# A two-block network on one core: expert weights laid out in other runs, three result buffers, the router tile by tile, the first group by a product

## The chip, the cores and the metric

The program runs on one core of a Trainium2 chip. The metric is the device time in microseconds of one execution, median of three runs. TensorE (PE) multiplies matrices, its weight loads stand apart as PEld; VectorE (DVE), ScalarE (ACT) and GpSimd (POOL) compute; SyncE (SP) only issues transfers. GpSimd and ScalarE issue some too.

## The reference, cut to what matters

A first block of two layers (a mixer or attention and an MLP each, on 256 tokens and 256 context rows of width 1024) comes first and is not touched. The second block ends in the mixture of experts that the change is about. All is in float32.

```
h2 = _rms(x, norm2_g) * (1.0 + sc2) + sh2
g_logits = h2 @ w_rg + b_rg                       # 4 groups
g_top = argmax(g_logits); gate_g = softmax(g_logits)[g_top]
e_in = (h2 @ w_re + b_re).reshape(-1, 4, 4)[g_top]  # 4 experts of that group
top_v, top_j = top_k(e_in, 2)                     # 2 of them
w_sel = softmax(top_v) * gate_g
for e in range(16):
    he = silu(h2 @ w1[e]) * (h2 @ w3[e])          # w1, w3: 1024 x 512
    y += combine[:, e:e+1] * (he @ w2[e])         # w2: 512 x 1024
x = x + g2 * y
```

## The kernel before

Five instruction streams, one for each engine, are written out by hand and held together by semaphores. PSUM's eight banks go round in order of use up to the experts, and there have fixed roles. Weights come over SyncE's queue.

Behind the second block's output projection (`out_project(2, ...)`) VectorE adds the residual to each of two token tiles and norms it into `xn` (`rms_row`). TensorE transposes both tiles (`turn_x("moe")`), ScalarE and VectorE write the scaled and shifted columns to `hT` (`modulate`), with the scales and shifts in `modc`, one column for each block of 128 features. Then come the gates' broadcast (`gate_rows`) and the router's product. VectorE picks two experts for each token, TensorE counts how many tokens each expert has before each token ("pos"), and VectorE works out for each token and choice a slot, `slot_i`. An expert has a home of 64 slots; up to 7 spill units of 64 slots take what goes over, and `table_i` says for which expert each of them is.

GpSimd waits for `slot_i` and scatters the rows of `xn` into `x_slots` in DRAM with four indirect transfers (`x_spread`). Then it loads groups of 128 slots, two units, back into `xs`. `turn_group` transposes such a group, `modulate_group` scales it into `hs`. 23 units run in this order: expert 0, expert 1, spill 0, expert 2, expert 3, spill 1 and so on, and last 14 and 15. So a round is two experts and a spill unit. For each unit, `up` multiplies by w1 and w3 (32 passes of 128x512 on half the array), ScalarE and VectorE make silu and product, `turn_he` turns the result, `down` multiplies by w2 (16 passes) and `keep_y` scales it into one of two `ysb` buffers. GpSimd stores each in `y_slots`, and waits for two stores back guard the buffers. In the program every float32 product is two passes, two MATMULs in the profile.

SyncE loads w1 and w3 of an expert into two halves of `wring`, by the expert's parity, as soon as the `up` two experts back is done; w2 likewise into `w2_ring`. Spill units have buffers of their own, and their loads carry a condition, so one that isn't needed moves nothing. The first spill load waits for the table and for the scatters, since it writes over `xn`. It is SyncE's next one behind experts 0 and 1, so all weights behind it wait too. `inverse_roots` on GpSimd makes the inverse roots of all norms, in order with its transfers; two of them belong to the index keys at the start of the second block, which `rel_bias`, `w_rg` and other small loads precede.

The last two units' results are added by TensorE (`add_late`) with one-hot picks (`pick_late`, `turn_picks`); the others are gathered from `y_slots`.

## Time and profile before

| | us |
|---|---|
| median of 3 runs (1724.14 to 1730.26) | 1725.04 |
| profiled execution | 1726.32 |
| its span in the trace | 1724.5 |
| TensorE busy | 1626.6 |
| VectorE busy | 697.5 |
| ScalarE busy | 256.0 |
| GpSimd busy | 108.3 |

All times below are from the start of the span of the one profiled execution. The experts' part runs from about 1396 to the end. "busy" counts neither waits nor the issue of transfers. A row of the timeline gives start, length, engine, line and instruction, then in brackets the idle time ahead of it and what ended it; "issue" there is a wait that no semaphore event of an engine explains. SPq is SyncE's queue of transfers.

### The profile page before, as it was taken

What the parts mean: (1) busy time and instruction counts of PE and PEld (TensorE: products, weight loads), DVE (VectorE), ACT (ScalarE), POOL (GpSimd) and SP (SyncE); (2) the same over time, 40 slices, a digit from 0 to 9 for tenths busy, and PEclk for the clock granted to TensorE, in tenths of its full rate; (3) what the DMA queues carried; (4) which work ended last, traced back from release to release, by engine and by line L of the source; (5) the groups of instructions that cost most, each with busy time, mean ns of one, the idle gap of its engine ahead of it and who ended that gap; (6) DMA issues with size and microseconds to landing.
All of it is one profiled execution on the core that took longest, in us unless ns stands there. A gap on an engine that the chain in (4) does not pass through costs nothing.

```text
span 1724.5 us, 17356 instructions
## 1 busy us (share of the span) xinstructions
PE 1626.6 (94%) x6960; PEld 878.5 (51%) x6960; DVE 697.5 (40%) x1322; ACT 256.0 (15%) x576; POOL 108.3 (6%) x123
## 2 busy tenths in 40 slices
PE   4999999999999999999989999999989958998997
PEld 2445556474444444446756788448855633333332
DVE  1617853468886000112264765004484342111112
ACT  3121113010000000000154110000222311011110
POOL 1000001100000000001000100001131110110101
PEclk9999999999999999999989999999999978999999
DMA  9452441146665321107610699424623449999996
GB/s 340 169 195 99 146 165 56 49 147 219 214 225 207 135 98 49 49 1 257 225 50 1 229 333 363 175 98 154 197 98 122 147 178 354 390 392 391 391 387 254
DMA packets 160623, 333.94 MB, mean 194 GB/s; under 512 B 15288, under 2 KB 15568, under 8 KB 160544
## 3 DMA queue, kind: packets, MB, share of 16 engines
q1 hardware_dynamic: 141408, 298.90, 47.7%
q0 software_dynamic: 18224, 30.78, 5.5%
q10 hardware_dynamic: 912, 3.17, 0.5%
q8 instruction: 55, 0.90, 0.2%
q14 instruction: 24, 0.20, 0.0%
HBM read 355.02 MB, written 15.48 MB: 215 GB/s over the span
## 4 chain that ended last, share of the span: by engine, by line
PE 88%; DMA 4%; DVE 4%; issue 2%; POOL 1%; ACT 1%; SPq 0%; DVEq 0%; ACTq 0%; POOLq 0%
PE psum L624 85%; PE psum L628 4%; DMA wring<-in_ev_w_in 2%; DMA wring<-in_w_mod 1%; DMA wring<-in_mlp_w 1%; ACT wide L1663 0%; POOL small L1523 0%; DVE wide L2068 0%; DVE big L2401 0%; DMA x_slots<-wide,slot_i 0%; DVE big L2560 0%; DMA big<-x_slots 0%; DVE small L2559 0%; POOL x_slots L1609 0%; DVE small L2183 0%
## 5 line engine op out<-in xcount | busy, mean ns | idle before, releaser
L624 PE MATMUL psum<-wring,big 128*128 128x512 f32 (+2 forms) x1600 | 559.6, 579 | 13.8 <-issue 13.3
L624 PE MATMUL psum<-wide,wring 128*128 128x256 f32 (+3 forms) x1872 | 490.2, 437 | 0.2
L624 PEld LDWEIGHTS psum<-wring,big 128*128 128x128 f32 (+1 forms) x1600 | 242.8, 173 | 310.1 <-issue 306.1
L624 PEld LDWEIGHTS psum<-wide,wring 128*128 128x128 f32 (+1 forms) x1872 | 304.3, 184 | 173.0 <-issue 144.6
L624 PE MATMUL psum<-wring,wide 128*128 128x512 f32 (+3 forms) x576 | 216.1, 576 | 9.0 <-DMA wring<-in_w_mod 5.4
L1663 ACT ACTIVATE big<-psum 128x512 f32<-128x512 f32 (+2 forms) x155 | 83.0, 546 | 665.0 <-PE psum L624 614.3
L2068 DVE SCALAR_TENSOR_TENSOR wide<-wring,csilu,wide 128x512 f32<-128x512 f32 x252 | 175.5, 748 | 3.0
L624 PEld LDWEIGHTS psum<-wring,wide 128*128 128x128 f32 (+1 forms) x576 | 97.7, 188 | 109.2 <-issue 96.0
L2168 DVE TENSOR_TENSOR wide<-psum,gate 128x512 f32<-128x512 f32 x27 | 18.7, 691 | 325.2 <-PE psum L624 325.0
L1523 POOL TENSOR_TENSOR small<-small 128x1 f32<-128x1 f32 (+2 forms) x30 | 41.1, 1372 | 1037.8 <-DVE small L2185 884.7
L1663 ACT ACTIVATE wide<-psum 128x256 f32<-128x256 f32 (+2 forms) x114 | 46.0, 418 | 313.3 <-PE psum L628 158.9
L624 PE MATMUL psum<-big,wide 128*64 128x512 f32 (+1 forms) x408 | 90.7, 566 | 0.0
L2836 DVE TENSOR_TENSOR wide<-wide,psum 128x256 f32<-128x256 f32 x23 | 9.7, 421 | 179.0 <-ACT wide L1663 179.0
L2068 DVE SCALAR_TENSOR_TENSOR big<-wring,csilu,big 128x512 f32<-128x512 f32 x112 | 74.9, 745 | 0.0
L2216 DVE TENSOR_TENSOR big<-big,psum 128x512 f32<-128x512 f32 (+1 forms) x62 | 35.1, 567 | 97.3 <-ACT big L1663 94.3
L1663 ACT ACTIVATE wide<-psum,modc 128x256 f32<-128x256 f32 (+1 forms) x36 | 16.2, 514 | 348.8 <-PE psum L628 348.6
L624 PE MATMUL psum<-big 128*64 128x128 f32 (+5 forms) x592 | 59.3, 328 | 7.7 <-ACT wide L1663 3.6
L624 PEld LDWEIGHTS psum<-big,wide 128*64 128x64 f32 (+1 forms) x408 | 30.8, 142 | 49.2 <-issue 48.3
L624 PE MATMUL psum<-wide,lnb 128*64 128x512 f32 x224 | 50.8, 595 | 0.0
L624 PEld LDWEIGHTS psum<-big 64*128 64x128 f32 (+2 forms) x592 | 41.6, 168 | 17.1 <-issue 15.6
L628 PEld LDWEIGHTS psum<-const,wide 128*128 128x128 f32 x214 | 24.9, 150 | 37.9 <-issue 25.5
L628 PE MATMUL psum<-const,wide 128*128 128x128 f32 x214 | 35.3, 300 | 5.6 <-DVE wide L2208 4.8
(266 smaller groups left out, 885.5 us busy)
## 6 DMA issues: line engine op xcount, KB each, us to landing
wring<-in_mlp_w SPq DMA_DIRECT2D x32, 2048.0 KB, 8.7
wring<-in_w SPq DMA_DIRECT2D x32, 2048.0 KB, 21.9
wring<-in_w_mod SPq DMA_DIRECT2D x24, 2048.0 KB, 13.0
big<-in_w SPq DMA_DIRECT2D x23, 2048.0 KB, 20.6
wide<-in_w SPq DMA_DIRECT2D x14, 2048.0 KB
wring<-in_w_ada SPq DMA_DIRECT2D x12, 2048.0 KB, 8.6
wring<-in_w_in SPq DMA_DIRECT2D x8, 2048.0 KB, 8.4
wring<-in_ev_w_in SPq DMA_DIRECT2D x6, 2048.0 KB, 13.0
```

Of the source, the lines that this page charges most:

```text
L624: return nc.tensor.matmul(o, a, b, start=first, stop=last)
L628: return nc.tensor.transpose(o, a, ident[0:n, 0:n])
L1523: nc.gpsimd.tensor_tensor(a, a, half_neg[:, 0:a.shape[1]], ALU.pow).then_inc(rate_done, 1)
L1663: return nc.scalar.activation(o, a, func, **kw)
L2068: ins = v_.scalar_tensor_tensor(acc, w, by, acc, ALU.mult, ALU.add)
L2168: free(v_.tensor_tensor(ubuf, bank(name), gate[:, gv, cs], ALU.mult), name)
L2216: free(v_.tensor_tensor(h, h, src, ALU.mult), name)
L2836: v_.tensor_tensor(he[:, i % 2, :], sg[:, i % 2, :], psum[:, i % 2, T:2 * T], ALU.mult).then_inc(he_ready, 1)
```

## The change

It has these parts.

1. w1 and w3 are dealt to the partitions another way: partition p gets rows 8p to 8p+7 instead of p, 128+p, ..., in two transfers of four rows, each 8 KB in one run, where there were eight runs of 2 KB. w2 comes as two runs of 8 KB a partition instead of four of 4 KB. So that the products are the same, the routed activations are dealt likewise: `rms_row(t, True)` writes `xn` with every eighth feature together, the scales and shifts come from a new `modp`, which takes a detour over DRAM, and `he` takes every second column. The router's weights are dealt too.
2. `ysb` has three buffers.
3. The router goes by token tile: transposes of tile 0 stand between the two halves of the last output projection, and the gates' rows behind the router.
4. The first group's slots (experts 0 and 1) are filled by a product of `xn` with a one-hot matrix `first_hot`, `gather_first`, not by scatter, load and transposes. The scatters stay. SyncE's first spill load waits for the gather too.
5. The picks of the last two units are made and turned behind the first group's modulation and the first `up`.

```diff
-        ysb = region(lnb_flat, 0, 2, 512)
+        ysb = (region(lnb_flat, 0, 512), region(lnb_flat, 512, 512), region(gate_flat, 1536, 512))
...
             out_project(2, yT2, (2,), turn_second)
-            out_project(2, yT2, (3,))
-
-            pe.wait_ge(xn_ready, 4)
-            turn_x("moe", xn, (0, 1))
+            out_project(2, yT2, (3,), lambda: turn_routed("moea", 0))
+            router("moea", 0)
+            turn_routed("moeb", 1)
+            router("moeb", 1)
             gate_rows(2, 1)
...
+            def gather_first():
+
+                pe.wait_ge(first_ready, 1)
+                for k in range(KC):
+                    for t in range(2):
+                        last = mm(psum[:, 4 + k // 4, (k % 4) * P:(k % 4 + 1) * P], xn[:, t, k * P:(k + 1) * P],
+                                  first_hot[:, t, :], t == 0, t == 1)
                 last.then_inc(xs_turned, 1)
...
-            turn_picks()
-            turn_group(GROUP_ORDER[0])
-            pe.wait_ge(late_ready, 1)
+            gather_first()
             for i in range(UNITS):
                 up(i)
+                if i == 0:
+                    turn_picks()
+                if i == 2:
+                    pe.wait_ge(late_ready, 1)
...
                 for w, src in enumerate((I["w1_2"], I["w3_2"])):
-                    sp.dma_start(w13_ring[e % 2][:, w], src[0, e].rearrange("(k p) n -> p k n", p=P)).then_inc(w13_in[e % 2], 16)
+                    for k in range(0, KC, 4):
+                        sp.dma_start(w13_ring[e % 2][:, w, k:k + 4],
+                                     src[0, e].rearrange("(p k) n -> p k n", p=P)[:, k:k + 4]).then_inc(w13_in[e % 2], 16)
...
-                sp.dma_start(w2_ring[:, e % 2], I["w2_2"][0, e].rearrange("(f p) n -> p f n", p=P)).then_inc(w2_in[e % 2], 16)
+                sp.dma_start(by_halves(w2_ring[:, e % 2]), I["w2_2"][0, e].rearrange("(h p c) n -> p h c n", h=2, c=2)).then_inc(w2_in[e % 2], 16)
...
                     sp.wait_ge(table_ready, 1)
                     sp.wait_ge(x_spread, 64)
+                    sp.wait_ge(xs_turned, 1)
...
             pool.wait_ge(x_ready, 12)
+            pool.wait_ge(modc_ready, 4)
+            for j in range(2):
+                pool.dma_start(modp_scratch[j].rearrange("(k p) -> p k", p=P), modc[:, 2, 24 + 8 * j:32 + 8 * j, 0],
+                               allow_slow_non_contiguous=True).then_inc(modp_out, 16)
...
+            pool.wait_ge(modp_out, 32)
+            pool.dma_start(modp[:, :, :], modp_scratch.rearrange("j (p k) -> p j k", p=P)).then_inc(modp_in, 16)
...
-            loaded = 0
+            loaded = 1
...
+            step(v_.tensor_scalar(first_slot, slot_f, float((NEXP - LATE) * SLOTS), None, ALU.add))
+            for t in range(2):
+                step(v_.tensor_scalar(first_hot[:, t, :], cst("late"), first_slot[:, 0, t:t + 1], None, ALU.is_equal))
+            for t in range(2):
+                last = v_.scalar_tensor_tensor(first_hot[:, t, :], cst("late"), first_slot[:, 1, t:t + 1], first_hot[:, t, :],
+                                               ALU.is_equal, ALU.add)
+            last.then_inc(first_ready, 1)
...
-                if i > 1:
-                    dve.wait_ge(y_stored[i % 2], 16 * (i // 2))
-                v_.tensor_tensor(ysb[:, i % 2, :], psum[:, 6 + i % 2, :], gy, ALU.mult).then_inc(ysb_ready, 1)
+                if i > 2:
+                    dve.wait_ge(y_stored[i % 3], 16 * (i // 3))
+                v_.tensor_tensor(ysb[i % 3], psum[:, 6 + i % 2, :], gy, ALU.mult).then_inc(ysb_ready, 1)
```

What TensorE has in a row from the last output projection to the first expert, first before. The names are those of the operands' buffers: `wring,big` 128x512 is the output projection, `const,wide` 128x128 transposes of `xn`, `const,modc` the gates, `small,wide` the router, `const,gate` the picks, `const,big` a group of slots, 64x512 an expert.

```order
278 L624 MATMUL psum<-wring,big 128x512 x24
279 L628 MATMUL psum<-const,wide 128x128 x16
280 L624 MATMUL psum<-const,modc 128x128 x8
281 L624 MATMUL psum<-small,wide 128x20 x16
282 L624 MATMUL psum<-lnb,const 128x32 x2
283 L628 MATMUL psum<-const,gate 128x128 x4
284 L628 MATMUL psum<-const,big 128x128 x8
285 L624 MATMUL psum<-wring,big 64x512 x24
```

And after, where `lnb,wide` 128x128 is `gather_first`:

```order
278 L642 MATMUL psum<-wring,big 128x512 x16
279 L646 MATMUL psum<-const,wide 128x128 x8
280 L642 MATMUL psum<-wring,big 128x512 x8
281 L642 MATMUL psum<-small,wide 128x20 x8
282 L646 MATMUL psum<-const,wide 128x128 x8
283 L642 MATMUL psum<-small,wide 128x20 x8
284 L642 MATMUL psum<-const,modc 128x128 x8
285 L642 MATMUL psum<-lnb,const 128x32 x2
286 L642 MATMUL psum<-lnb,wide 128x128 x16
287 L642 MATMUL psum<-wring,big 64x512 x16
288 L646 MATMUL psum<-const,gate 128x128 x4
```

Half of the transposes moved between the projection's halves, the router split in two, the gates went behind it, and the picks went behind the first unit's products.

GpSimd's transfers at the start of the second block, before:

```order
34 L1523 TENSOR_TENSOR small<-small 128x1 x4
35 L1557 DMA small<-in_rel_bias 32x8
36 L1557 DMA big<-in_const_buckets 32x511
37 L1565 DMA big<-in_q_norm_g 64x1 x2
38 L1565 DMA big<-in_k_norm_g 64x1 x2
39 L1565 DMA small<-in_w_rg 128x8x4
40 L1565 DMA small<-in_w_re 128x8x16
41 L1565 DMA small<-in_b_rg 128x4
42 L1565 DMA small<-in_b_re 128x16
43 L1569 DMA wide<-in_const_levels 128x1920
44 L1523 TENSOR_TENSOR small<-small 128x1 x2
```

And after:

```order
34 L1567 TENSOR_TENSOR small<-small 128x1 x4
35 L1602 DMA modp_scratch<-modc 128x8x1 x2
36 L1605 DMA small<-in_rel_bias 32x8
37 L1605 DMA big<-in_const_buckets 32x511
38 L1613 DMA big<-in_q_norm_g 64x1 x2
39 L1613 DMA big<-in_k_norm_g 64x1 x2
40 L1613 DMA small<-in_w_rg 128x8x4
41 L1613 DMA small<-in_w_re 128x8x16
42 L1613 DMA small<-in_b_rg 128x4
43 L1613 DMA small<-in_b_re 128x16
44 L1615 DMA modp<-modp_scratch 128x2x8
45 L1619 DMA wide<-in_const_levels 128x1920
```

Two stores stand ahead of these loads now, and the reload of `modp` stands behind them, ahead of the levels table and the two index-key roots.

## Rows read from the trace of the kernel before

**Rows 1.** The page, its 40 slices of 43.1 us: the DMA engines.

```profile
DMA  9452441146665321107610699424623449999996
```

**Rows 2.** Windows: length, busy us (instructions) by engine, then clock, DMA share, GB/s.

```profile
1400.00:1420.00 20.00, 7.69 (x51) 7.44 (x50) 10.02 (x55) 2.31 (x3) 2.06 (x2) 0.59 0.56 215
1420.00:1440.00 20.00, 9.91 (x38) 4.79 (x40) 6.79 (x24) 3.76 (x8) 3.61 (x5) 0.60 0.85 309
...
1480.00:1500.00 20.00, 20.00 (x98) 7.13 (x96) 2.90 (x7) 3.04 (x8) 0.83 (x1) 1.00 1.05 386
```

**Rows 3.** Timeline, one round of the experts, and the last scaling: start, us, what.

```profile
1469.44 3.65 PE L624 MATMUL psum<-wring,big 128*64 128x512 f32 x16
...
1478.68 3.65 PE L624 MATMUL psum<-wring,big 128*64 128x512 f32 x16 [2.15 <-issue]
...
1505.44 3.65 PE L624 MATMUL psum<-wring,big 128*64 128x512 f32 x16
...
1712.57 0.69 DVE L2831 TENSOR_TENSOR lnb<-psum,gate 128x512 f32<-128x512 f32 x1 [5.67 <-PE psum L624]
```

**Rows 4.** Waits from 1340 on: us in total, times, longest.

```profile
DVE lnb L2831 <- PE psum L624: 58.7, 23, 5.7
...
PE psum L624 <- issue: 13.3, 7, 2.4
```

**Rows 5.** Timeline from the normed tile to the first expert product.

```profile
1395.19 0.75 DVE L2208 TENSOR_SCALAR wide<-xres,small 128x1024 f32<-128x1024 f32 x1 [0.67 <-POOL small L1523]
...
1399.47 3.18 PE L624 MATMUL psum<-const,modc 128*128 128x128 f32 x16
...
1402.49 4.15 PE L624 MATMUL psum<-small,wide 128*128 128x20 f32 x32
...
1406.74 0.20 DVE L2730 TENSOR_TENSOR small<-psum,small 128x40 f32<-128x40 f32 x1 [5.96 <-PE psum L624]
...
1416.33 0.17 DVE L2784 CAST slot_i<-lnb 128x4 int32<-128x4 f32 x1
...
1420.49 0.16 DVE L2799 TENSOR_REDUCE small<-small 128x2 f32<-128x8 f32 x1 [1.69 <-ACT small L1663]
...
1426.64 1.09 PE L628 MATMUL psum<-const,gate 128*128 128x128 f32 x4 [13.81 <-DVEq L2818]
1427.04 1.02 SPq L1470 DMA_DIRECT2D wide<-in_w  x2
...
1429.54 1.97 PE L628 MATMUL psum<-const,big 128*128 128x128 f32 x8 [1.80 <-DMA big<-x_slots]
...
1431.55 1.50 ACT L1663 ACTIVATE big<-psum,modc 128x128 f32<-128x128 f32 x4 [3.12 <-PE psum L628]
...
1433.15 12.00 PE L624 MATMUL psum<-wring,big 128*64 128x512 f32 x48 [1.64 <-issue]
...
1441.75 10.33 SPq L1449 DMA_DIRECT2D wring<-in_w  x3
```

**Rows 6.** DMA view of 1440 to 1690: queue, packets, MB, share of 16 engines.

```profile
q1 hardware_dynamic: 36555, 87.28, 92.6%
```

**Rows 7.** DMA view of 1357 to 1370, weights in 2 KB packets alone.

```profile
q1 hardware_dynamic: 1999, 4.06, 88.3%
```

**Rows 8.** DMA view of 1719 to 1724, the stores of the output alone.

```profile
q10 hardware_dynamic: 288, 1.05, 52.5%
```

**Rows 9.** DMA view of 1209.8 to 1216, the queue that loads the levels table.

```profile
q0 software_dynamic: 226, 1.00, 57.6%
```

**Rows 10.** Timeline around GpSimd's loads for the second block.

```profile
1206.80 0.94 POOL L1565 DMA_DIRECT2D small<-in_w_rg  x1
...
1214.72 0.20 DVE L2525 COPY big<-big 128x64 f32<-128x64 f32 x1
...
1220.19 0.44 PE L628 MATMUL psum<-const,big 128*128 128x128 f32 x2
...
1226.81 0.94 POOL L1578 DMA_DIRECT2D gate<-rel_scratch  x1 [4.98 <-DMA rel_scratch<-big]
```

More of the change, by code:

```diff
@@ L229, in build @@
         modrows = sb("modrows", [P, P])
+        modp = sb("modp", [P, 2, KC])
         slot_i = sb("slot_i", [P, 4], I32)
@@ L544, in build @@
         ysb_ready = sem("ysb_ready")
-        y_stored = [sem(f"y_stored{a}") for a in range(2)]
+        y_stored = [sem(f"y_stored{a}") for a in range(3)]
         pick_ready = sem("pick_ready")
@@ L591, in build, with shift_of, scale_of @@
                  "mlp1a": (1, 1, 0, 0, 1, 3), "mlp1b": (1, 1, 0, P, 1, 3), "mix2a": (2, 0, 0, 0, 1, 4), "mix2b": (2, 0, 0, P, 1, 4),
-                 "moe": (2, 1, 0, 0, 2, 4)}
+                 "moea": (2, 1, 0, 0, 1, 4), "moeb": (2, 1, 0, P, 1, 4)}
+        def shift_of(part, k):
+            l, half, v = PARTS[part][:3]
+            return modp[:, 0, k:k + 1] if (l, half) == (2, 1) else modc[:, l, 24 * half + k, v:v + 1]
+        def scale_of(part, k):
+            l, half, v = PARTS[part][:3]
+            return modp[:, 1, k:k + 1] if (l, half) == (2, 1) else modc[:, l, 24 * half + 8 + k, v:v + 1]
         def banks_of(part):
@@ L1292, in turn_second, with turn_routed, router @@
                 turn_y(2, mix, 1, 1)
+            def turn_routed(part, t):
+                pe.wait_ge(xn_ready, 3 + t)
+                turn_x(part, xn, (t,))
+            def router(part, t):
+                wait_h(part)
+                o = claim(f"router{t}")
+                for k in range(KC):
+                    last = mm(o[:, 0:20], hT[:, k, t * P:(t + 1) * P], wr[:, k, :], k == 0, k == KC - 1)
+                last.then_inc(bank_full, 1)
             out_project(2, yT2, (2,), turn_second)
-            out_project(2, yT2, (3,))
-            pe.wait_ge(xn_ready, 4)
-            turn_x("moe", xn, (0, 1))
+            out_project(2, yT2, (3,), lambda: turn_routed("moea", 0))
+            router("moea", 0)
+            turn_routed("moeb", 1)
+            router("moeb", 1)
             gate_rows(2, 1)
-            wait_h("moe")
-            o = claim("router")
-            for t in range(2):
-                for k in range(KC):
-                    last = mm(o[:, t * 20:(t + 1) * 20], hT[:, k, t * P:(t + 1) * P], wr[:, k, :], k == 0, k == KC - 1)
-            last.then_inc(bank_full, 1)
             pe.wait_ge(ind_ready, 1)
@@ L1694, in modulate @@
                 act.wait_ge(modc_ready, done)
+                if (l, half) == (2, 1):
+                    act.wait_ge(modp_in, 16)
                 width, per = n * P, 4 // n
@@ L1701, in modulate @@
                         last = f(hT[:, k, at:at + width], bank(name)[:, j * width:(j + 1) * width], ACT.Identity,
-                                 bias=modc[:, l, 24 * half + k, v:v + 1], scale=modc[:, l, 24 * half + 8 + k, v:v + 1])
+                                 bias=shift_of(part, k), scale=scale_of(part, k))
                     free(last, name)
@@ L2140, in modulate @@
                 l, half, v, at, n, done = PARTS[part]
+                if (l, half) == (2, 1):
+                    dve.wait_ge(modp_in, 16)
                 width, per = n * P, 4 // n
@@ L2147, in modulate @@
                         last = v_.tensor_scalar(hT[:, k, at:at + width], bank(name)[:, j * width:(j + 1) * width],
[L2148 to L2149 removed]
+                                                scale_of(part, k), shift_of(part, k), ALU.mult, ALU.add)
                     free(last, name)
@@ L2793, in _, with modulate_group @@
             signal(v_.tensor_copy(table_i[:, :], table_f.rearrange("p a n -> p (a n)")), table_ready)
-            rt_x4 = rt_exp.rearrange("p (t e) -> p t e", t=2)
-            step(v_.tensor_tensor(rt_x4[:, :, 0:4], lg[:, :, 0:4], each(rt_g), ALU.subtract))
-            signal(v_.tensor_tensor(rt_x4[:, :, 4], rt_2, rt_1, ALU.subtract), route_ready)
+            def modulate_group(g):
+                dve.wait_ge(xs_turned, GROUP_AT[g] + 1)
+                for k in range(4, KC):
+                    last = v_.tensor_scalar(slots_of(g)[:, k, :], psum[:, 5, (k - 4) * P:(k - 3) * P], modp[:, 1, k:k + 1],
+                                            modp[:, 0, k:k + 1], ALU.mult, ALU.add)
+                last.then_inc(hs_ready, 1)
+            modulate_group(0)
             dve.wait_ge(route_exp, 1)
```

87 lines of the change are left out of this document (50 added, 37 removed).

## The prediction, made before the changed kernel was run

> **What bounds the kernel now.** I read the page's slices first: the DMA engines are full only over the last seventh [rows 1]. That is the mixture of experts, so I read it by windows [rows 2]: from 1400 to 1440 TensorE is busy 17.6 of 40 us at a clock of 0.6; in a window like that from 1480 it is busy throughout and the DMA engines have a share of 1.05 at 386 GB/s. So there are two things to look at: a start in which everything waits for the router and the dispatch, and a long stretch in which TensorE and the weight stream are almost equally long.
>
> The timeline shows the second in one round (two experts and one spill unit, which is how the order repeats): the like product starts at 1469.44 and at 1505.44, so a round takes 36.0 us, and 2.15 us of it is a gap before the products of an odd expert [rows 3]. The buffers, banks and vectors of that unit are long there, so I read the gap as waiting for its w1 and w3. The list of waits has seven such gaps, 13.3 us [rows 4]; one (1.64 us, before the first product at 1433.15 [rows 5]) is ScalarE's modulation, 1431.55 and 1.50, so six gaps, 11.7 us, are DMA. Take them out and the chain from 1433.15 to the last scaling at 1712.57 [rows 3, 5] is 279.4 - 11.7 = 267.7 us of TensorE work, some 34 us a round. The weight stream needs 36.0. It is the bound, by 2 us a round.
>
> **What a packet costs.** The stream's own queue moved 36555 packets, 87.28 MB, in 92.6% of 16 engines for 250 us: 101.3 ns for 2.39 KB on average, and all queues together have 1.05 of the engines [rows 2, 6]. Where only 2 KB packets move, 1999 take 88.3% of 16 x 13 us: 91.9 ns [rows 7]. The stores of the output, 4 KB packets, take 52.5% of 16 x 5 us over 256 of them: 164 ns [rows 8]. The straight line through both is 20 ns a packet and 36 ns a KB. It gives 104 ns at the stream's mean size, where 101.3 was measured, so I take 90 ns for a 2 KB packet within the stream. No row shows an 8 KB packet there. The line gives 308 ns; twice a 4 KB packet is 328. I take 312, near the line, since it met the third point.
>
> **The change, part by part.**
> *Packets.* A round carries 8.39 MB of w1 and w3 in 4096 packets of 2 KB, 23.0 us of 16 engines; as 1024 of 8 KB 20.0. Its w2, 1024 packets of 4 KB, 10.5; as 512 of 8 KB 10.0. That is 3.5 us, over 1.05 is 3.3: the stream's round falls from 36.0 to 32.7 (34.1 at 328 ns). TensorE's stays at 34. So TensorE becomes the bound, and of 3.3 us only 2 are worth anything. Late next is nothing but TensorE itself.
>
> The same splitting costs SyncE twice as many issues of w1 and w3, but each has 128 runs instead of 1024, and it waits for the ring anyway.
>
> *Router tile by tile.* Before, xn of the second tile is ready at 1395.94, 16 transposes, the gates and 32 router passes follow, and the logits are read at 1406.74 [rows 5]. After, eight transposes of tile 2 stand between the last two halves of the output projection: +1.0 us for all behind them at full clock (eight at half take 1.97, [rows 5]). The dealt xn reads every eighth element: 0.75 us for 1024 elements now, 1.28 us for an operation of one element a cycle (the two ends); I take +0.4. xn is ready at 1397.4. Eight transposes at half clock 1.85, four modulations of 128 columns 1.4 and 0.1 on either side: 1400.9. Sixteen router passes, 4.15/2 = 2.1 at best, 3.2 if all at half clock; 2.6. The logits are read at 1403.6, 3.1 earlier. The gates stand behind the router now, in time that TensorE has until the counts.
>
> *First group by a one-hot product.* slot_i is done at 1416.5, so then 1413.4. A shift and four comparisons of 128 columns at 0.3: 1414.9. Sixteen products, 32 passes of 128 columns: gate rows of that shape took 3.18 for 16 passes, mostly at half clock, so 6.4; at the router's 0.13 a pass 4.2. I take 6.4, since the granted clock is 0.60 here [rows 2]. Then ScalarE's modulation, as now, 1.6. The first expert product starts at 1423.0 instead of 1433.15: **-10.2**. The four scatters leave this path but stay in the program, for the other groups and for SyncE; one reload and eight transposes go.
>
> *Picks.* VectorE's 6.2 us of gates and picks (1420.49 to TensorE's 1426.64 [rows 5]) move behind its modulation. They end at 1423.0 + 6.2 = 1429.2, under the first product, which lasts to 1431.6 (8.6 us now, up to SyncE's issue at 1441.75, which waits for it). Four transposes enter the chain: **+0.5**. With cover gone they'd cost up to 6.
>
> *Start of the stream.* SyncE's first issue behind the scatters is at 1427.04 [rows 5], then 3.1 earlier; that it also waits for the gather, which ends at 1421.4, adds nothing. The first starved product is at 1478.68, 51.6 us into the stream. Of this, the x load that is no longer made is 0.52 MB, 1.3 us; the 14.7 MB of weights before it save (34.6 + 5.3) - (30.0 + 5.0) = 4.9, over 1.05 4.6. The weights land at 1478.7 - 3.1 - 1.3 - 4.6 = 1469.7. TensorE is there at 1476.5 - 10.2 + 0.5 = 1466.8. It waits **+2.9** once; after that the stream gains 1.3 us a round on TensorE. The other gaps go: **-11.7**.
>
> *Third result buffer.* VectorE's 23 scalings wait for TensorE alone [rows 4]: 0, hidden by the time that two units take, 24 us.
>
> *modp.* GpSimd gets three more transfers: two of 1024 four-byte runs (0.94 us to issue, as for w_rg of 1024 runs) and a reload that waits for their landing. The store of rel_scratch landed within 5.0 us [rows 10]; ten issues of 0.5 to 0.9 us lie between these stores and GpSimd's wait, so it waits 0 to 2 us. With the three issues the root behind it moves by 3 to 5 us. VectorE's two index keys hang on it and are done at 1214.9, TensorE turns them at 1220.19: 5.2 us of cover. I take 0; with the cover gone each us costs one.
>
> **Sum.** -10.2 + 0.5 - 11.7 + 2.9 = -18.5. The profiled execution took 1726.3 with a span of 1724.5; it would be 1707.8 with 1706.0. The median of the runs, 1725.04, lies 1.3 below the profiled one: 1706.5.
>
> **Rivals.**
> *The stream gains little.* If only a quarter of the 20 ns is the packet's own and the rest the ramp of one window, an 8 KB packet takes 345 ns, and a round falls by (23.0 - 22.1 + 10.5 - 10.35)/1.05 = 1.0 to 35.0: the stream stays the bound. The end moves by the start, 3.1 + 1.3, and 7 x 1.0: 1713.6 by the median. For it: the line rests on two windows, and the first holds a ramp. Against it: the point between them fits within 3%. Chance 0.12. The Trainium skill has a rule of this kind, on the page "DMA: Bandwidth & Descriptors", in the section on why small descriptors are slow: about 3 cycles of 32 bytes a packet, so 67 cycles for the 64 of a 2 KB packet; a 2 KB packet would carry 4% and not 22% of overhead, and an estimate from it is a round shorter by 0.9 and an end near 1714. The rows of this trace show more. No gain at all, since 386 GB/s may be a ceiling: -4.4, 1720.5; against it 2 KB windows show the lower rate per engine. Chance 0.08.
> *Slower: large packets in a pitch of 16 KB.* Two neighbouring partitions' reads, before 2 KB apart, are 16 KB apart. The only packets near that size, the levels table at 1209.8, took 57.6% of 16 x 6.2 us for 1.00 MB, 57 ns a KB against 45 for 2 KB packets [rows 7, 9]; but they shared the engines with the stream. Break-even: a round may grow by 0.6 us, 356 ns a packet; at 403 ns a round takes 41 and the end is 1760. It takes all the start's gain with it, since the stream decides. Chance 0.07. The same page's table of measured facts warns of slow copies at row pitches that are large powers of two, from 512 KiB up; no run here shows one, and 16 KB is far below.
> *Better.* If the clock holds through the short gaps, the gather takes 4.2 and the router 2.1, and the first starvation is partly covered: about 1701. Chance 0.08.
> *modp too late.* If the four-byte stores take over 10 us, TensorE waits at 1220: 1710 to 1716. Chance 0.05.
> The forecast itself: 0.60, range 1700 to 1712.
>
> **How the numbers follow.** A measurement of this kernel can tell about 0.5%, 8.6 us: faster means below 1716.4. Forecast, better, modp and most of small gain lie there: 0.60 + 0.08 + 0.05 + 0.10 = 0.83. No gain and the rest of small gain: 0.10. Pitch: 0.07. The range leaves out the no gain and pitch cases: 1698 to 1717.
>
> **What would show it.** Packets of 8192 bytes, mean near 312 ns; about 13,000 of them for the 106 MB of 17 experts. First expert product near 1423, logits near 1403.6. From then a round of 34 us, DMA share of the last stretch below 1.0, and gaps before odd experts gone but for one of some 3 us. If the rounds still take 36, the packets' price is wrong; if they take 34 but the end is late, the start is. No wait of TensorE before the turned index keys at 1220 clears modp. What would make the prediction wrong is above all a packet price off the line, since every round hangs on it.

## The result: 1712.4 us, 0.5% faster, where 1706.5 was forecast

| | before | after |
|---|---|---|
| median of seven runs, us | 1725.04 | 1712.39 |
| lowest and highest | 1716.22 to 1730.26 | 1708.83 to 1717.91 |
| ratio, 95% interval | | 0.9947 [0.9924, 0.9969] |
| profiled execution and its span | 1726.32, 1724.5 | 1712.39, 1710.6 |

The direction and the range held. The gain did not: 12.6 us by the medians and 0.53% by the ratio, where 18.5 us or 1.07% were forecast, so two thirds of it by the one and half of it by the other. In the spans 4.6 us are missing, 1710.6 against the forecast 1706.0, and the rows say where.

The windows at the start of the experts, of the changed kernel (length, busy us by engine, then clock, DMA share, GB/s), answer to [rows 2]:

```profile
1400.00:1420.00 20.00, 11.52 (x54) 10.78 (x52) 11.94 (x63) 4.06 (x8) 3.02 (x3) 0.59 0.65 271
1420.00:1440.00 20.00, 18.34 (x97) 7.84 (x96) 7.53 (x26) 4.54 (x9) 2.12 (x3) 1.00 0.80 304
1440.00:1460.00 20.00, 15.69 (x76) 5.38 (x74) 4.54 (x11) 3.78 (x10) 2.82 (x4) 1.00 1.02 415
1460.00:1480.00 20.00, 18.39 (x80) 6.17 (x82) 1.11 (x2) 1.15 (x3) 0.84 (x1) 0.91 1.02 416
1480.00:1500.00 20.00, 20.00 (x98) 6.88 (x94) 3.59 (x8) 2.66 (x7) 2.21 (x3) 1.00 1.02 406
```

TensorE is busy 18.3 of the 20 us from 1420, at full clock, where it had 9.9 at 0.60. The engines that move data carry 406 to 416 GB/s at a share of 1.02, where they carried 386 at 1.05. The hole from 1440 to 1480, 5.9 us of idle time, was forecast at 2.9. It stands before the products of expert 2; the forecast had it one unit later, before expert 3.

TensorE's timeline of the changed kernel, from the second tile's transposes to the first expert product, and then its waits in the experts' part ([rows 3, 5] before):

```profile
1399.08 1.52 PE L646 MATMUL psum<-const,wide 128*128 128x128 f32 x8 [3.25 <-DVE wide L2266]
1402.21 3.58 PE L642 MATMUL psum<-small,wide 128*128 128x20 f32 x16 [1.61 <-ACT wide L1713]
...
1416.88 5.33 PE L642 MATMUL psum<-lnb,wide 128*128 128x128 f32 x32 [5.30 <-DVE lnb L2850]
1423.87 7.09 PE L642 MATMUL psum<-wring,big 128*64 128x512 f32 x32 [1.66 <-ACT big L1713]
...
1461.61 5.04 PE L642 MATMUL psum<-wring,big 128*64 128x512 f32 x16 [5.92 <-issue]
...
1665.56 1.09 PE L646 MATMUL psum<-const,big 128*128 128x128 f32 x8 [1.63 <-DMA big<-x_slots]
```

Two gaps are left: 5.92 us at 1461.61, where TensorE has used up the weights on hand, and 1.63 us at 1665.56 for a group of slots, which is new. The six gaps before odd experts are gone: the list of waits from 1340 on has TensorE waiting once for "issue", against seven times and 13.3 us [rows 4].

```profile
PE psum L642 <- issue: 5.9, 1, 5.9
...
PE psum L646 <- DMA big<-x_slots: 1.6, 1, 1.6
```

The DMA view of 1480 to 1640 of the changed kernel (packets, MB, share of 16 engines; then KB each and median us from issue to landing), and below it the same stretch of the kernel before:

```profile
q1 hardware_dynamic: 7936, 58.77, 89.5%
...
big<-x_slots POOLq DMA_DIRECT2D x7, 512.0 KB, 25.3
y_slots<-lnb POOLq DMA_DIRECT2D x10, 256.0 KB, 23.1
```

```profile
q1 hardware_dynamic: 23015, 55.58, 91.9%
...
y_slots<-lnb POOLq DMA_DIRECT2D x13, 256.0 KB, 12.6
big<-x_slots POOLq DMA_DIRECT2D x6, 512.0 KB, 15.5
```

58.77 MB are 7174 packets of 8 KB (the other 762 are of a few bytes). 89.5% of 16 x 160 us over 7174 is 319 ns a packet; 312 was forecast. But the two kinds of transfer on GpSimd's queue, which the change does not touch, take nearly twice as long to land.

GpSimd's timeline around the new detour of the modulation row, and what TensorE does meanwhile ([rows 10] before):

```profile
1201.15 2.20 POOL L1602 DMA_DIRECT2D modp_scratch<-modc  x2
...
1208.79 0.55 POOL L1613 DMA_DIRECT2D small<-in_b_re  x1
1213.26 0.71 POOL L1615 DMA_DIRECT2D modp<-modp_scratch  x1 [3.92 <-DMA modp_scratch<-modc]
1214.24 0.55 POOL L1619 DMA_DIRECT2D wide<-in_const_levels  x1 [0.27 <-issue]
1214.81 0.57 POOL L1567 TENSOR_TENSOR small<-small 128x1 f32<-128x1 f32 x1
```

```profile
1206.53 7.36 PE L642 MATMUL psum<-wide,wring 128*128 128x128 f32 x64
...
1216.91 0.30 PE L646 MATMUL psum<-const,big 128*128 128x128 f32 x1 [2.08 <-DVE big L2583]
1219.56 0.47 PE L646 MATMUL psum<-const,big 128*128 128x128 f32 x1 [2.35 <-DVE big L2583]
1220.85 2.08 PE L642 MATMUL psum<-big 64*128 64x128 f32 x16 [0.81 <-ACT big L1713]
```

GpSimd stands at its wait for the scattered stores for 3.92 us, issues the reload, and only at 1214.81 makes the root for which VectorE has waited 10.12 us. TensorE waits twice for the index keys, 2.08 and 2.35 us, 4.4 together. The first row there is the index queries' 64 products, at a granted clock of 1.00; in the kernel before they took 9.51, at 0.76:

```profile
1209.81 9.51 PE L624 MATMUL psum<-wide,wring 128*128 128x128 f32 x64
```

### The profile page after: what moved, and what is told of

Its sections match the earlier page's. It is cut to its first block, busy times and chain, and to the rows that moved or that the text cites. A ratio compares the mean times of both kernels' runs of the same rounds, so it can differ in the third digit from the quotient of the medians.

```text
span 1710.6 us, 17491 instructions
## 1 busy us (share of the span) xinstructions
PE 1627.8 (95%) x6984; PEld 880.4 (51%) x6984; DVE 700.6 (41%) x1332; ACT 257.3 (15%) x580; POOL 110.4 (6%) x125
## 4 chain that ended last, share of the span: by engine, by line
PE 86%; DMA 5%; DVE 4%; issue 2%; POOL 1%; SPq 1%; ACT 1%; DVEq 0%; POOLq 0%; ACTq 0%
PE psum L642 82%; PE psum L646 3%; DMA big<-x_slots 2%; DMA wring<-in_w_mod 1%; DMA wring<-in_mlp_w 1%; SPq L1474 1%; DMA y_slots<-gate 1%; DMA wring<-in_ev_w_in 1%; POOL small L1567 1%; ACT wide L1713 0%; DMA wide<-y_slots,slot_i 0%; DVE wide L2122 0%; DVE big L2459 0%; DVE big L2618 0%; ACT big L1713 0%
## 5 line engine op out<-in xcount | busy, mean ns | idle before, releaser
L646 PE MATMUL psum<-const,big 128*128 128x128 f32 (+1 forms) x204 | 28.0, 279 | 16.0 <-DMA big<-in_b_ada 8.5
## 6 DMA issues: line engine op xcount, KB each, us to landing
big<-in_w SPq DMA_DIRECT2D x23, 2048.0 KB, 23.1
```

The source lines that it names most:

```text
L646: return nc.tensor.transpose(o, a, ident[0:n, 0:n])
```

## The experiments

The theory: what is missing is the modulation row's detour ahead of the experts and a late start of the weight stream, while the packets do as forecast. The rivals: the packets bring less than they seem to, or the gather does. The kernels were measured in four groups after the first result, each on one chip with its own runs of the kernel before: the changed kernel again, the late modulation row, the packets alone and the start alone; then the early spilled load, no gather, two result buffers and 4 KB packets; then the last two pairs. Ratios and medians of one group can be set side by side, those of two groups only roughly. All ratios are to the kernel before. Where an expectation speaks of the gap before expert 3, the products behind the gap are those of expert 2.

### The changed kernel again

> The changed kernel once more, to stand beside the others on one chip. Expected from the record: a ratio to the kernel before of 0.993 to 0.995, and in the trace a first expert product 24 to 26 us behind the second normed tile, one gap of 5 to 6 us before expert 3's products, and two gaps of some 2 us before the turned index keys near 1215 to 1220.

Measured: 1711.52 us (1708.59 to 1714.28), ratio 0.9931 [0.9918, 0.9943]. In its profile the waits for the index keys are 1.41 and 2.35 us, and the gap in the experts is 4.26 us. So both are there in both profiled executions of this kernel, and the 5.9 us of the first is not the usual size: the kernels below that start the stream in the same way with 8 KB packets and the gather show 3.6 to 4.2.

### The modulation row behind the small loads

```diff
-            for j in range(2):
-                pool.dma_start(modp_scratch[j].rearrange("(k p) -> p k", p=P), modc[:, 2, 24 + 8 * j:32 + 8 * j, 0],
-                               allow_slow_non_contiguous=True).then_inc(modp_out, 16)
...
-            pool.wait_ge(modp_out, 32)
-            pool.dma_start(modp[:, :, :], modp_scratch.rearrange("j (p k) -> p j k", p=P)).then_inc(modp_in, 16)
...
             pool.dma_start(rowg[:, 1, :], I["attn_out_g_2"].to_broadcast([P, 512])).then_inc(rowg_in, 16)
+            for j in range(2):
+                pool.dma_start(modp_scratch[j].rearrange("(k p) -> p k", p=P), modc[:, 2, 24 + 8 * j:32 + 8 * j, 0],
+                               allow_slow_non_contiguous=True).then_inc(modp_out, 16)
+            pool.wait_ge(modp_out, 32)
+            pool.dma_start(modp[:, :, :], modp_scratch.rearrange("j (p k) -> p j k", p=P)).then_inc(modp_in, 16)
```

> The changed kernel with modp's two stores and its reload moved behind GpSimd's loads of the norm gains, well past the two index-key roots. Theory 1 (modp holds GpSimd, 3.9 us in the wait for the stores and some 3 us of issues, and TensorE waits 2.1 and 2.4 us for the index keys): both TensorE gaps near 1215 go, the time falls by 3 to 4 us against the changed kernel. Rival (the gaps come from TensorE's clock having been higher there in that one trace): gaps of TensorE near 1215 stay or the time stays within 1 us.

Measured: 1706.09 us (1700.2 to 1710.96), ratio 0.9897 [0.9877, 0.9917], beside the 0.9931 above: 5.4 us by the medians, somewhat more than expected. TensorE's timeline of this kernel at the same place:

```profile
1214.50 1.02 PE L642 MATMUL psum<-big,small 32*8 32x511 f32 x2
1215.45 0.44 PE L646 MATMUL psum<-const,big 128*128 128x128 f32 x2
1216.69 1.16 PE L642 MATMUL psum<-big 64*128 64x128 f32 x16 [0.81 <-ACT big L1713]
```

The two transposes of the index keys stand right behind the product ahead of them, without a wait, and the sixteen products behind take 1.16 us at a granted clock of 1.00, where those of the changed kernel take 2.08 at 0.50: the clock that the waits had cost is there as well. The detour is shown to cost what the forecast put at nothing.

How much it costs depends on the clock of the execution, and the move does not set that clock. From the product of 128x72 to the first of 128x256 behind the index keys, the five profiled kernels whose row stands late took 12.39 us twice and 15.64 us three times; in the latter the 64 products took 9.4 to 9.7 us, as in the kernel before, and not 7.36. The seven profiled executions with the detour in front took 16.8 to 18.3. So the detour costs 4 to 6 us where the clock is full, and against an execution with the slow products it would be 1 to 3, an estimate from these rows.

With the detour out TensorE comes to the experts sooner and waits for weights four times, 7.0 us in all, the longest 3.91. The stream is not far from being the bound again.

### The packets alone

The kernel before, with nothing but the new loads of w1, w3 and w2. The activations are not dealt to match, so the experts multiply other pairs of rows.

```diff
-                    sp.dma_start(w13_ring[e % 2][:, w], src[0, e].rearrange("(k p) n -> p k n", p=P)).then_inc(w13_in[e % 2], 16)
+                    for k in range(0, KC, 4):
+                        sp.dma_start(w13_ring[e % 2][:, w, k:k + 4],
+                                     src[0, e].rearrange("(p k) n -> p k n", p=P)[:, k:k + 4]).then_inc(w13_in[e % 2], 16)
...
```

> The kernel before with nothing changed but the weight transfers, 8 KB runs; its experts' rows stand in another order than the activations, so its experts' result is not the reference's. Theory 1 (the weight stream's six gaps were the stream's own rate, and the packet price of 312 to 320 ns lifts it over TensorE's round of 34 us): first expert product where it was, 1433, all gaps before odd experts gone, 10 to 12 us less than before, ratio 0.993 to 0.994, so nearly the whole gain of the change. Rival (most of the change's gain is the earlier start): a gain of 0 to 4 us.

Measured: 1715.72 us (1708.9 to 1721.96), ratio 0.9942 [0.9919, 0.9965]: 7.8 us by the medians, where 10 to 12 were expected. The six gaps are gone, at 410 GB/s. From its first product, 1429.97, to the last scaling at 1702.09 it takes 272.1 us, against 279.4 [rows 3, 5]. Taking out the gaps should have left 267.7. What came in their place, 4.4 us, is the second row here, the group of slots:

```profile
DVE lnb L2839 <- DMA y_slots<-lnb: 106.4, 15, 11.0
...
PE psum L628 <- DMA big<-x_slots: 5.9, 3, 3.8
```

VectorE, with two result buffers, now waits for their stores 15 times, 106.4 us in all, where it waited for TensorE alone before [rows 4]. TensorE has slack for that and does not wait. It does wait 5.9 us for x_slots, of which 1.6 stand before its first expert product, as 1.8 did before; the other two waits, 0.51 and 3.84 us, lie in the experts' part and are new.

### The start alone

The changed kernel with the old runs of 2 and 4 KB. Here too the experts multiply other pairs.

```diff
-                    for k in range(0, KC, 4):
-                        sp.dma_start(w13_ring[e % 2][:, w, k:k + 4],
-                                     src[0, e].rearrange("(p k) n -> p k n", p=P)[:, k:k + 4]).then_inc(w13_in[e % 2], 16)
+                    sp.dma_start(w13_ring[e % 2][:, w], src[0, e].rearrange("(k p) n -> p k n", p=P)).then_inc(w13_in[e % 2], 16)
...
```

> The changed kernel with the weight transfers of the kernel before (2 KB and 4 KB runs); again the rows stand in another order, so the experts' result is not the reference's. Theory 1 (the stream decides the end, and it starts at 1427 in both): the early start of TensorE at 1424 is given back in a longer first gap, rounds of 36 us as before, total within 2 us of the kernel before or up to 3 us slower for modp. Rival (the start is worth its 9 us by itself): 6 to 9 us below the kernel before.

Measured: 1726.71 us (1717.79 to 1733.0), ratio 1.0014 [0.9998, 1.0031]. The end comes no earlier. But this kernel carries the modulation row's detour too, and that must be taken out of the reading. Its timeline from the second tile's norm to the first starvation:

```profile
1401.44 1.14 DVE L2262 TENSOR_SCALAR wide<-xres,small 128x1024 f32<-128x1024 f32 x1 [0.67 <-POOL small L1563]
1427.85 7.09 PE L642 MATMUL psum<-wring,big 128*64 128x512 f32 x32 [1.65 <-ACT big L1709]
1431.19 1.02 SPq L1510 DMA_DIRECT2D wide<-in_w  x2
1456.02 3.65 PE L642 MATMUL psum<-big,wide 128*64 128x512 f32 x16
1470.10 6.20 PE L642 MATMUL psum<-wring,big 128*64 128x512 f32 x16 [10.42 <-issue]
```

From the end of that norm to the first expert product it takes 25.3 us, against 37.2 in the kernel before [rows 5]: 11.9 us earlier. Of this TensorE gives back 5.8 in the experts, which take 285.2 us to the last scaling instead of 279.4: one wait of 10.42 us and four of 1.3 to 1.7 (16.4 us in all), where there were six with 11.7. With 2 KB packets the stream decides, and behind the norm it starts only 2.5 us earlier than before (28.6 us against 31.1). Some 6 us are left at the last scaling, and the stretch ahead of the norm, with the detour in it, is 5.9 us longer: 195.0 us from the product of 128x72 to the norm's end, against 189.1.

The medians of this group (the kernel before 1723.54) say the same in other numbers: the packets alone bring 7.8 us, the start alone costs 3.2, and together they bring 12.0. If the detour costs its 5.4 us here too, which was not run with small packets, the start is worth some 2 us with 2 KB packets (5.4 - 3.2) and some 10 with 8 KB (12.0 - 7.8 + 5.4). So the two halves of the change are not a sum.

### 4 KB packets

```diff
-                    for k in range(0, KC, 4):
+                    for k in range(0, KC, 2):
...
```

with runs of 4 KB for w2 as before, in the changed kernel. Only w2 does not match its activations.

> The changed kernel with 4 KB runs for all expert weights, w1 and w3 in pieces of two rows; w2's rows stand in another order than the activations, so the experts' result is not the reference's. By the line through 92 ns at 2 KB and 164 ns at 4 KB a round of the stream is 34.2 us against TensorE's 34: gaps of 0 to 1 us a round, the first gap 1 us longer, 1 to 4 us above the changed kernel. Rival (only 8 KB runs help): rounds of 36 us and a time as with the old packets, 12 to 15 us above it. Landing of the result stores: 22 us if large packets of the other queue hold them up, between 13 and 22 at 4 KB.

Measured: 1717.63 us (1712.5 to 1721.07), ratio 0.9971 [0.9955, 0.9986]. The DMA view of 1480 to 1640:

```profile
DMA packets 23326, 64.11 MB, mean 401 GB/s; under 512 B 7708, under 2 KB 7708, under 8 KB 23317
...
big<-x_slots POOLq DMA_DIRECT2D x6, 512.0 KB, 16.5
y_slots<-lnb POOLq DMA_DIRECT2D x9, 256.0 KB, 14.4
```

So 390, 401 and 410 GB/s at 2, 4 and 8 KB, and landing times of GpSimd's transfers that stay near the old ones at 4 KB and nearly double only at 8. The ratio follows the rate: 1.0014, 0.9971, and 0.9931 and 0.9947 in the two groups with the changed kernel. With 4 KB TensorE waits for weights 7.3 and 2.7 us.

### Without the gather

The changed kernel, but the first group comes by scatter, reload and transposes, as before.

```diff
-            gather_first()
+            turn_group(GROUP_ORDER[0])
...
-                    sp.wait_ge(xs_turned, 1)
...
-            loaded = 1
+            loaded = 0
```

> The changed kernel with the first group again scattered, reloaded and turned; the one-hot matrix is still made, nobody uses it. Theory 1 (of the 9 us that the start gained, 6 to 7 were given back in the gap before expert 3): first product some 9 us later, gap gone, time only 1 to 4 us above the changed kernel. Rival (the start counts in full): 8 to 10 us above it.

Measured: 1719.9 us (1714.94 to 1722.39), ratio 0.9979 [0.9966, 0.9992]; the two other kernels of that group with the gather and 8 KB packets stand at 0.9906 and 0.9944. The first product is at 1432.56 instead of 1423.87, 8.7 us later; the hole of 5.9 us is gone; the waits for x_slots in the experts' part are 5.0 us (4.51 of it at 1672.91) instead of 1.6; and the first unit's 32 products take 9.80 us instead of 7.09, while the 1.4 us of clock behind the hole are saved. That makes 8.7 - 5.9 + 3.4 + 2.7 - 1.4 = 7.5 us. From the norm's end to the last scaling the profile has 307.4 us, against 299.3 and 298.3 in the two of the changed kernel, so 8 to 9. The medians say 5.9 against the two-buffer kernel of the same group, and 5.5 to 8.3 by the ratios of the changed kernel in other groups. The gather is worth 6 to 9 us, between the two sizes expected or at the larger; the runs do not tell it more closely. In the profile 3.4 us of it are not the start but the later groups' loads.

The run shows something else. GpSimd's wait for the scatters:

```profile
1425.10 1.16 POOL L1667 DMA_DIRECT2D big<-x_slots  x2 [3.39 <-DMA x_slots<-wide,slot_i]
```

It is 3.39 us, as with the packets alone (3.37) and in the kernel before (3.40), while in the six kernels with the gather and without an early load it is 4.7 to 5.0. The transfers up to that point are the same.

### Two result buffers

```diff
-        ysb = (region(lnb_flat, 0, 512), region(lnb_flat, 512, 512), region(gate_flat, 1536, 512))
+        ysb = (region(lnb_flat, 0, 512), region(lnb_flat, 512, 512))
```

with the counts of its semaphores by 2 instead of 3.

> The changed kernel with two result buffers. In its trace the stores take 22 to 24 us to land where they took 12.6, and a buffer comes round after two units, 23 us. Theory 1 (the third buffer is needed because of the larger packets): VectorE's scaling waits for a landing in most units, TensorE for VectorE one unit later only where it lasts over 10 us, so 0 to 4 us more. Rival (as the prediction had it): no wait anywhere, same time within 1 us.

Measured: 1714.03 us (1710.2 to 1717.3), ratio 0.9944 [0.9922, 0.9966]. VectorE waits for stores 12 times, 73.5 us. Against the changed kernel's 0.9931 and 0.9947 in other groups this is no difference that these runs can tell.

### The first spilled load early

SyncE waited, ahead of the first spilled expert's loads, for the scatters and the gather, since w3's part of the spill buffer lies over `xn`. w1's does not.

```diff
                 if n == 0:
                     sp.wait_ge(table_ready, 1)
-                    sp.wait_ge(x_spread, 64)
-                    sp.wait_ge(xs_turned, 1)
...
                 for w, src in enumerate((I["w1_2"], I["w3_2"])):
+                    if n == 0 and w == 1:
+                        sp.wait_ge(x_spread, 64)
+                        sp.wait_ge(xs_turned, 1)
                     for k in range(0, KC, 4):
```

> The changed kernel in which the first spill expert's w1 (2 MB, into the half of the buffer that no scatter reads) is loaded as soon as the table is there, ahead of the wait for the scatters and the gather. Theory 1 (the first starvation, 5.9 us plus 1.4 us of half clock behind it, comes from a stream that starts at 1427 while TensorE starts at 1424): the stream starts near 1420, some 5 us of data earlier, the gap before expert 3 shrinks from 5.9 to 0 to 2 us, time 4 to 6 us less than the changed kernel. Rival (the scatters and the first loads share the engines, so the scatters end later by as much): gap and time as in the changed kernel.

Measured: 1706.32 us (1704.69 to 1710.31), ratio 0.9906 [0.9888, 0.9925]. The hole is smaller, though not down to the 0 to 2 us expected, in TensorE's timeline:

```profile
1469.80 3.65 PE L642 MATMUL psum<-wring,big 128*64 128x512 f32 x16 [2.83 <-issue]
```

and GpSimd's shows what it costs: its wait for the scatters is 7.80 us, not 4.90, as it is 7.6 to 8.4 in the three other profiles with this load. That the scatters now share the engines with the stream is the plain reading; it was not tested by itself.

```profile
1429.10 1.16 POOL L1668 DMA_DIRECT2D big<-x_slots  x2 [7.80 <-DMA x_slots<-wide,slot_i]
```

No changed kernel ran in this group. Against its ratios in the others this one is 0.0025 and 0.0041 lower, 4 to 7 us.

### Both moves, and the loads of the groups further ahead

The first is the two moves together. The second issues each later group's load two places earlier in GpSimd's queue:

```diff
-                while loaded < GROUPS and (loaded < 2 or begins[loaded - 2] <= i + 1):
+                while loaded < GROUPS and (loaded < 2 or begins[loaded - 2] <= i + 3):
```

> The changed kernel with two moves of steps: the modulation row's two stores and its reload stand behind the router's small row loads on GpSimd's queue, and the first spilled expert's first weight load is issued on SyncE ahead of its wait for the scatters. Each was run alone: 0.9897 and 0.9906 of the kernel before, against 0.9931 and 0.9947 for the change itself. Theory (the two lost times are apart, one lies before the first scatter and the other behind it): they add, 0.9931 - 0.0034 - 0.0025 to 0.004 gives 0.986 to 0.988, about 1700 us by a kernel before of 1723; the waits for the index keys are gone, and behind the first eight products one gap of 2 to 4 us stays, for the second weights. Rival (an earlier stream start only lengthens the scatters, so TensorE starts later by as much): the two together give 0.989 to 0.991, no better than either alone, and the first product comes later than 1419 us.

> The kernel of the run before this one, with each later group's load from x_slots issued two places further ahead in GpSimd's queue. Theory (the load lands late because its 4 KB packets stand beside 8 KB ones for some 25 us, and the group is needed then): the wait of 1.6 to 4.5 us for x_slots near 1665 us goes, the time is 0.001 to 0.0025 lower in ratio than that of the run before. Rival 1: the groups' loads then wait for the turn of the group before, and hold back the stores of the results behind them on GpSimd's queue, so VectorE waits for a result buffer and TensorE for VectorE; same or up to 5 us slower. Rival 2: the time does not change, because another load is late at the same place.

Measured side by side: 1705.82 us (1702.15 to 1711.25), ratio 0.9925 [0.9900, 0.9950], and 1703.80 us (1699.03 to 1708.85), ratio 0.9907 [0.9881, 0.9933]. The moves together missed what was expected of them by 0.005 and came out no better than the late modulation row by itself (0.9897), although the profile has their signs: no wait for index keys, two gaps of 1.55 and 2.25 us in place of one of 5.9, and a span of 1700.4. Nor is it the rival, which wanted a first product later than 1419 us: it is at 1415.36. The kernel before had a median of 1720.5 in this group, 1.3 to 4.5 below the others, which may be part of the miss; the rest stays open. The earlier loads moved by 0.0018, as expected, inside the intervals: the gap for x_slots (1.62 us in the first) is gone, and x_slots lands in 14.6 us instead of 25.0. The stores behind it pay, 28.2 us instead of 24.0, and VectorE waits for them six times, 25.6 us, with three buffers.

To tell whether the early spilled load adds anything, the kernel with all three moves ran beside the one without it:

> The kernel that had all three moves (0.9907), with the early first spilled load taken back: the modulation row late and the groups' loads two places ahead are left. Theory (the three gains lie at three places and add): 0.001 to 0.003 above the kernel with all three in the same call, and behind the first eight products two gaps of 4 to 6 us together in place of 1.6. Rival (what the early spilled load gains behind the first products it gives back ahead of them: with it the second tile's transposes began a chain that reached the first product 0.9 us later): the two kernels come out within 0.001 of each other.

> The kernel with all three moves once more, beside the one without the early spilled load. Theory: 0.987 to 0.989, lower than that one by 0.001 to 0.003, no gap for x_slots, and 269 to 271 us from the first product of the experts to the last scaling. Rival: 0.990 to 0.991, as the kernel beside it.

Measured: without it 1708.38 us (1706.39 to 1713.36), ratio 0.9917 [0.9893, 0.9941]; with it 1701.78 us (1697.49 to 1705.7), ratio 0.9874 [0.9847, 0.9901]. It adds 0.004, more than expected. The profiles show little of it: the gap is 4.18 us without it and 2.20 and 0.98 with it, and from first product to last scaling it is 272.2 against 271.0 us, 1.2 of the 6.6 us between the medians. The profile without it also began the experts 6.3 us later (1426.23 against 1419.93), though up to there the two kernels are the same, so a good part of the 6.6 may be the spread of executions. All five runs with it are shorter than all six without. Against that stands the pair before, where the early load put on top of the late modulation row brought nothing that shows (0.9925 against 0.9897, in different groups). So that it helps is likely and not settled. The kernel with all three moves was the best of its group both times, 0.9874 and 0.9907; the late modulation row alone had 0.9897 in another.

## Why the prediction was right in kind and too high in its gain

Two terms of the sum failed. The modulation row's detour, put at 0, costs 5.4 us; the first starvation, put at +2.9, was 5.9. The parts in order:

**The packet's price: right.** 319 ns measured, 312 forecast. Four packets of 2 KB at 91.9 ns [rows 7] are 368, so a packet of 8 KB is 13% cheaper for its bytes. Rounds of two experts and a spill unit took 34.1 us on average over five, 34 forecast. The rivals in which the stream gains little or nothing are out, and that of the 16 KB pitch too. The Trainium skill, "DMA: Bandwidth & Descriptors", section "Why small descriptors are slow (HBM only)", has a fixed overhead of about 3 cycles a packet; an estimate from it is 3% from 2 to 8 KB, and the runs show four times that.

**The gaps: right, with a new one behind them.** All six are gone. "Late next is nothing but TensorE itself" was the wrong step: the groups of x_slots were late next, 1.6 us in the changed kernel and 4.4 in the experts with the packets alone, and their load takes 25.3 us where it took 15.5. Issued two places ahead, it is waited for no more.

**The first starvation: wrong in size.** 2.9 us forecast, 5.9 measured, and the sixteen products behind it took 5.04 us instead of 3.65, at a granted clock of 0.72 over those products. The step that failed is "SyncE's first issue behind the scatters is at 1427.04 [rows 5], then 3.1 earlier". The issue itself came at 1427.27, in this row:

```profile
1427.27 1.94 SPq L1513 DMA_DIRECT2D wide<-in_w  x4
```

That is 3.3 us later than forecast. 1.6 of it is the second tile's norm, which ends at 1399.02 and not at 1397.4 (the detour, below). Another 1.5 is the scatters' landing, at 1425.88 behind a wait of 4.90 us, where a kernel without the gather waits 3.4. So the gather delays by 1.5 us the very scatters that the stream waits for. That it is the gather is shown by the kernel without it; by what way was not tried. The early spilled load confirms that the late start costs: with it the wait for weights is 2.8 us instead of 5.9 and 4.3.

The place was wrong too. The forecast moved the first gap of the kernel before, at expert 3, and did not ask about expert 2, whose products had no wait there (1465.54, 38.5 us behind the stream's first issue). With TensorE 10 us earlier it is expert 2 whose weights are late first, 34.3 us behind that issue. TensorE has then paid, and expert 3's products at 1473.87 wait for nothing. For the size this matters little: with the stream's start as forecast, 1423.9, and the same 34.3 us, expert 2 would have waited some 2.4 us, an estimate. The late start is what makes it 5.9.

**modp at nothing: wrong, the largest miss.** The step reads "ten issues of 0.5 to 0.9 us lie between these stores and GpSimd's wait, so it waits 0 to 2 us" and "5.2 us of cover. I take 0". It waited 3.9 us (2.6 to 4.1 in the six other profiles with the detour in front), because the 2048 stores of four bytes, issued from 1201.15 on, are waited for until 1213.26: 12.1 us from the first issue, 10.8 to 12.3 over the seven profiles, and not the 5.0 of the store that was taken as the nearest row. And the cover was read from a stretch in which TensorE ran partly at half clock: the index queries' 64 products took 9.51 us before. At full clock they take 7.36, so TensorE is at the keys sooner and the cover shrinks by itself: in the kernel with the row late, which ran at full clock there, the second key is done at 1213.23 and TensorE turns it at 1215.45, which is 2.2 us and not 5.2. Taken out, the detour gives 5.4 us back. With it out the ratio is 0.9897, which is the forecast's 1.07% nearly whole. That is in part luck: in the profile of that kernel the experts take 2.3 us more than forecast, and the stretch from the product of 128x72 to the norm's end, at full clock, 3.3 us less. The rival "modp too late", given 0.05, describes what happened, and its 1710 to 1716 holds the 1712.4.

**The start: right.** From the end of the second tile's norm, 1399.02, to the first product, 1423.87, it takes 24.85 us; 25.6 were forecast. The gather took 5.33 (6.4 forecast), the dealt norm 1.14 (1.15), but the second tile's router product 3.58 (2.6), so the sum is nearer than its terms. The first product was late by 0.9: 1.6 at the norm's end, less 0.7 here. The 1.6 is the detour's cost less 2.2 us by which this execution's first block was ahead (the product of 128x72 starts at 1204.71, before at 1206.89).

**The third buffer: right at 0 us, for a wrong reason.** "VectorE's 23 scalings wait for TensorE alone" was true of stores that land in 12.6 us. They land in 23, and two buffers then make VectorE wait 73.5 us, which TensorE's own queue of work hides.

The 4.6 us of the span add up: 0.9 before the first product; 3.3 in the experts (3.0 of starvation, 1.4 of clock behind it, 1.6 for x_slots, and 2.7 less elsewhere, of which 1.5 is the first product of all, 7.09 us at full clock where 8.6 was carried over from before); 0.4 in the tail.

## What to carry to other kernels

When two parts of a change meet in one queue, ask of each which engine it sets free and whether that engine decides: the earlier start was worth some 2 us while the stream decided and some 10 once it didn't. When a part of the change makes the work arrive earlier, look for the first wait anew, and not only at the wait that was first before. And before a kernel with half of the change is called worth nothing, count what else it carries. A cover read from a stretch at half clock is not there once a change, or chance, lets the clock rise; convert it to full clock before leaning on it. Larger packets on one queue lengthened what was small on another here, so list the transfers of the other queues that have a deadline, and issue them earlier.

## What had not been expected of the hardware

Transfers of a queue with 2 to 4 KB in a packet take longer to land beside 8 KB packets of another queue, though their bytes stay as they were and the engines' total share nearly so (1.05 and 1.02): 256 KB stores 12.6, 14.4 and 23.1 us beside packets of 2, 4 and 8 KB, 512 KB loads 15.5, 16.5 and 25.3. The two halves of the change say the same apart: 22.4 and 24.9 us with the packets alone, 13.3 and 16.2 with the start alone. The Trainium skill, "DMA: Bandwidth & Descriptors", section "Queues, rings and completion order", says that each engine goes round its queues and takes a packet of several descriptors from each before the next. That fits the direction. The size does not follow a straight line in the packet's bytes: at 4 KB the times lie near those at 2. Nor is the neighbour's packet all: the same loads, issued two places ahead, landed in 14.0 to 15.1 us beside 8 KB packets in three kernels, and the stores then took 28. What decides was not settled.

The transfers of this one core, nine tenths of them weights, came to 410 GB/s. The Trainium skill, "HBM Reference", section "Specifications (TRN2)", gives about 425 for a core that streams alone; the runs agree within 4%.
